# Norms by quarters: an encoder layer whose next stage begins on half of the early transposed pieces

## The reference

```python
x = layer_norm(ALPHA * x + 0.5 * swiglu(x, ffn1_w_up, ffn1_w_down), ln1_g, ln1_b)
h = mixer(x, ...)     # x @ w_in, short convolution, retention with 4 heads, gates, @ w_out
x = layer_norm(ALPHA * x + h, ln2_g, ln2_b)
x = layer_norm(ALPHA * x + 0.5 * swiglu(x, ffn2_w_up, ffn2_w_down), ln3_g, ln3_b)
```

## Time and profile before

| | |
|---|---|
| median of 3 runs | 1802.85 us (1801.83 to 1803.66) |
| the profiled execution itself | 1801.98 us, span 1799.8 us |
| PE busy | 1777.6 us, 99% |
| DVE, ACT, POOL busy | 1281.2, 645.0, 541.1 us |
| chain that ended last | PE 91%, DMA 3%, POOL 1%, DVE 1%, ACT 1% |
| granted PE clock | 0.997 of full speed |

### The profile page before, as it was taken

One profiled execution on the slowest core, in us unless ns is written; L12 is line 12 of the kernel. 1 busy time (PEld: TensorE's weight loads), 2 busy tenths in 40 slices (PEclk: granted clock), 3 DMA queues, 4 the chain that ended last, 5 costly groups with the idle time before them and its releaser, 6 DMA issues.

```text
span 1799.8 us, 26971 instructions
## 1 busy us (share of the span) xinstructions
PE 1777.6 (99%) x10868; PEld 1656.8 (92%) x10868; DVE 1281.2 (71%) x1698; ACT 645.0 (36%) x1102; POOL 541.1 (30%) x360
## 2 busy tenths in 40 slices
PE   9999999999999999999999999999999999999997
PEld 8989899898999999999998979798989989899896
DVE  7958485667798787776257666767867868485675
ACT  5425233242545454544106050514205325242242
POOL 2324242224232222121341323232244324233231
PEclk9999999999999999999999999999999999999998
DMA  7342423325443333422764958586964332323313
GB/s 272 129 141 71 141 73 132 123 71 199 146 143 127 115 130 101 143 87 91 273 240 140 339 200 312 204 284 231 345 258 158 129 135 77 129 82 129 114 63 106
DMA packets 89419, 287.33 MB, mean 160 GB/s; under 512 B 8784, under 2 KB 11216, under 8 KB 89040
## 3 DMA queue, kind: packets, MB, share of 16 engines
q1 hardware_dynamic: 48176, 171.72, 28.3%
q0 software_dynamic: 15552, 56.63, 9.2%
q10 hardware_dynamic: 25568, 57.26, 8.7%
HBM read 244.35 MB, written 42.28 MB: 159 GB/s over the span
## 4 chain that ended last, share of the span: by engine, by line
PE 91%; DMA 3%; POOL 1%; issue 1%; DVE 1%; ACT 1%; DVEq 0%; POOLq 0%
PE ps L771 90%; DMA wh<-in_weights 2%; PE ps L1141 1%; POOL wl L684 1%; DMA wh_x<-in_weights 1%; ACT xh L1282 0%; POOL wl_x L684 0%; DVE y L2075 0%; DVE z L2064 0%; PE ps L1084 0%; DVE y L2084 0%; ACT xin L1282 0%; DVE rt L1682 0%; DVE xl L1682 0%; DVE mv L2070 0%
## 5 line engine op out<-in xcount | busy, mean ns | idle before, releaser
L771 PE MATMUL ps<-th,wql 128*128 128x320 f32 x1136 | 350.9, 309 | 0.0
L771 PE MATMUL ps<-th,wqh 128*128 128x320 f32 x1136 | 350.7, 309 | 0.0
L771 PE MATMUL ps<-tl,wqh 128*128 128x320 f32 x1136 | 350.0, 308 | 0.0
L684 POOL TENSOR_TENSOR wl<-raw,wh 128x1024 fp32r<-128x1024 f32 x101 | 257.3, 2549 | 97.7 <-DMA wh<-in_weights 70.6
L1282 ACT ACTIVATE pu<-ps 128x320 f32<-128x320 f32 x213 | 93.3, 438 | 522.7 <-PE ps L771 522.6
L1682 DVE TENSOR_TENSOR wql<-qraw,wqh 128x512 fp32r<-128x512 f32 x213 | 259.9, 1220 | 17.3 <-ACT wqh L1282 17.1
L771 PE MATMUL ps<-xl,wqh 128*128 128x320 f32 x852 | 262.7, 308 | 0.0
L771 PE MATMUL ps<-xh,wqh 128*128 128x320 f32 x852 | 262.6, 308 | 0.0
L771 PE MATMUL ps<-xh,wql 128*128 128x320 f32 x852 | 262.5, 308 | 0.0
L697 POOL TENSOR_TENSOR quad_s<-qraw 128x512 f32<-128x512 f32 x71 | 93.7, 1319 | 485.2 <-DVE wql L1682 449.0
L1682 DVE TENSOR_TENSOR wql<-quad_s,wqh 128x512 fp32r<-128x512 f32 (+1 forms) x213 | 194.3, 912 | 45.3 <-ACT wqh L1282 44.5
(11 more groups left out here) (221 smaller groups left out, 3440.8 us busy)
## 6 DMA issues: line engine op xcount, KB each, us to landing
qraw<-in_quads SPq DMA_DIRECT2D x142, 512.0 KB, 3.6
raw<-in_weights SPq DMA_DIRECT2D x105, 512.0 KB, 3.8
wh<-in_weights POOLq DMA_DIRECT2D x101, 512.0 KB, 5.5
state<-in_state_ret ACTq DMA_DIRECT2D x32, 512.0 KB, 6.7
out_ret_sample<-state ACTq DMA_DIRECT2D x32, 512.0 KB, 5.2
state<-in_state_ret SPq DMA_DIRECT2D x16, 512.0 KB, 5.3
qk_scratch<-ctp SPq DMA_DIRECT2D x8, 640.0 KB, 5.4
swish_scratch<-ctp SPq DMA_DIRECT2D x6, 640.0 KB, 3.0
```

The lines of the kernel that those rows point to most:

```text
L684: pool.tensor_tensor(w_lo(r), w_raw(r), w_hi(r).bitcast(f32), ALU.subtract).then_inc(chunk_split, 1)
L771: ins = nc.tensor.matmul(out, lhs, rhs, start=start, stop=stop, skip_group_check=adds)
```

## The change

`FIRST_UNITS` goes from 3 to 4: four first halves stand ahead of the second halves, and the late tiles are transposed at k = 5 of the fourth unit. The idle products at the norms go. The early pieces are transposed in another order, and the first unit begins when the q = 0 pieces have high parts (`x_high`), with its products sorted by part. The first quad's operands are made inside the norm: POOL makes all four weight sums (`all_sums`) before the norm, ACT the six high parts, DVE the low parts at other places. The release order at the first norm, the place of one extra chunk slot, and the time of two quad loads and of two reloads of `z_kept` change with it.

```diff
-FIRST_UNITS = 3
+FIRST_UNITS = 4
-LATE_AT = (FIRST_UNITS - 1, 7)
+LATE_AT = (FIRST_UNITS - 1, 5)
-DOWN_LATE, OUT_LATE = (2, 0, 1, 3), (1, 0, 3, 4, 2)
-EXTRA_SLOT = {SECOND - DOWN_PARTS + 2: NSPL, SECOND: NSPL,
+DOWN_LATE, OUT_LATE = (3, 0, 2, 1), (1, 0, 3, 4, 2)
+EXTRA_SLOT = {SECOND - 1: NSPL, SECOND: NSPL,
+EARLY_PIECES = [(0, 0), (1, 0), (0, 1), (1, 1), (2, 0), (2, 1)]
+HIGH_ORDER = [(0, 0), (1, 0), (0, 1), (2, 0), (1, 1), (2, 1)]
+LOW_ORDER = [(t, q) for q in range(2) for t in range(EARLY)]
...
# SP, ahead of ffn(1)'s chunks (before: after its first three)
+            sync.wait_ge(merged_ready, KT)
+            for slot in range(4):
+                sync.wait_ge(state_out[slot], 32 * H)
+            load_quad(2)
+            load_quad(2)
             ffn(1)
...
# POOL
+            def all_sums(stage):
+                n = qk.at
+                sums(stage)
+                pool.wait_ge(pool_sums, 2 * n + 1)
+                pool.tensor_tensor(qs[:, 1, :], qs[:, 0, :], quad_source(n, A11), ALU.add).then_inc(later_sums, 1)
+                pool.wait_ge(later_sums, 2 * n + 1)
+                pool.wait_ge(quad_ready, operand(n - 1, S4))
+                pool.tensor_tensor(qs[:, 3, :], qs[:, 1, :], quad_source(n, A12), ALU.add).then_inc(later_sums, 1)
...
-                pool.wait_ge(z_ready, TT)
                 low()
+                pool.wait_ge(t_ready, 4 * 1 + 4)
                 sums(1)
...
             low()
+            all_sums(2)
             ffn(1)
...
# PE, to_T
-                if pieces is EARLY_PIECES:
-                    pe.wait_ge(x_low, kept + 1)
-                    pe.wait_ge(x_kept, kept + 1)
-                    idle_products(IDLE_UNITS, bk(-2 * EARLY) % 8)
+                if pieces is EARLY_PIECES:
+                    pe.wait_ge(psum_free, bk(EARLY - TT))
...
# PE, first_units
+                pe.wait_ge(x_kept, kept + 1)
+                for q in range(2):
+                    ks = range(4 * q, 4 * q + 4)
+                    pe.wait_ge(x_high, kept + HIGHS_BEFORE[q])
+                    for k in ks:
+                        products(0, 0, k, (0, 0), k == 0, False)
+                    pe.wait_ge(x_low, kept + EARLY * (q + 1))
+                    for k in ks:
+                        products(0, 0, k, (0, 1), False, False)
+                assert chunk() == s0
+                for k in range(KT):
+                    products(0, 0, k, (1, 0), False, k == KT - 1)
...
# ACT, end of the output product
+            act.wait_ge(psum_full, bk(EARLY))
+            for t in range(EARLY, TT):
+                kept_load(t)
+            for what in (A11, S12, A12, S3, A22, S4):
+                quad_hi_part(QUAD_START[2], what)
...
# DVE, x_sums: the wait for the first unit's chunk now stands before the second sum
+                    dve.wait_ge(chunk_used, released((SECOND, LAST)[stage - 1]))
                 tt(t3, b22, b12, ALU.subtract).then_inc(t_summed, 1)
...
# DVE, end_stage(k, ...)
+                if k == 1:
+                    quad_lo_part(PROJ, A11)
+                    quad_lo_part(PROJ, S12)
                 for t in early:
                     down(scale, 0, [t], residual)
                     moments(0, [t])
+                if k == 2:
+                    for what in (A11, S12, A12, S3, A22, S4):
+                        quad_lo_part(QUAD_START[2], what)
                 for t in early:
                     down(scale, 1, [t], residual)
                     moments(1, [t])
```

More of the change, by code:

```diff
@@ L1054, in ffn @@
                     idle_products(IDLE_START, 0)
-                for u in range(0 if first else FIRST_UNITS, 4):
-                    unit_of_chunk(x_wait=x_piece if first and u == 0 else None)
+                for u in range(FIRST_UNITS if first else 0):
+                    unit_of_chunk(x_wait=x_piece if u == 0 else None)
                 n = 0 if first else QUAD_START[2]
@@ L1103, in first_units, with products @@
                 own, kept = bk.at, (zr.at - EARLY) * 2
[L1104 to L1109, removed]
+                used = []
+                def products(u, half, k, which, start, stop):
+                    s, c = used[u], slice(half * HALF, (half + 1) * HALF)
+                    w_part, x_part = which
+                    w_of, x_of = (w_hi(s), w_lo(s))[w_part], (xh, xl)[x_part]
+                    return mm(ps[:, (own + 2 * u + half) % 8, 0:HALF], cols(k, 128, w_of), x_of[:, k, c], start, stop)
                 def late_tiles():
@@ new lines, in first_units @@
+                for u in range(FIRST_UNITS):
+                    pe.wait_ge(x_kept, kept + 2 * EARLY + u + 1)
+                    for k in range(KT):
+                        if u == 0 and k % 4 == 0:
+                            pe.wait_ge(x_low, kept + 2 * EARLY + (TT - EARLY) * (k // 4 + 1))
+                        products(u, 1, k, (1, 0), k == 0, False)
+                        products(u, 1, k, (0, 1), False, False)
+                        last = products(u, 1, k, (0, 0), False, k == KT - 1)
+                    last.then_inc(psum_full, 2)
+                    owed[0] = True
@@ L1331, in window @@
                 bk.add(2)
-                quad_hi_part(n, A11)
-                quad_hi_part(n, S12)
+                if ffn == 0:
+                    quad_hi_part(n, A11)
+                    quad_hi_part(n, S12)
                 plain_hi(2 * ffn)
-                for what in (A12, S3, A22, S4):
-                    quad_hi_part(n, what)
+                if ffn == 0:
+                    for what in (A12, S3, A22, S4):
+                        quad_hi_part(n, what)
                 act.wait_ge(psum_free, bk())
@@ L1483, in projections @@
                 x_hi_parts(1)
[L1484 to L1485 removed]
                 act.wait_ge(z_saved, 32)
[L1487 to L1492 removed]
+                for m in range(4):
+                    unit_gate(yr[:, m, :])
                 for q in range(len(PROJECTIONS)):
@@ L1659, in _ @@
         def _(dve):
-            bk, ad, st, hr, zr, root, lo = (Count() for _ in range(7))
+            bk, ad, st, hr, zr, root, lo, xc = (Count() for _ in range(8))
             V = nc.vector
@@ L1902, in projections @@
                 banks_freed(4)
-                for what in (A11, S12, A12, S3, A22, S4):
-                    quad_lo_part(n, what)
+                quad_lo_part(n, A22)
+                quad_lo_part(n, S4)
                 second_sum(n + 1)
@@ L2045, in end_stage @@
                 down(scale, 1, late, residual)
-                bk.add(2 * EARLY)
-                transposed_freed(k, early)
                 if residual is z:
```

202 lines of the change are left out of this document (111 added, 91 removed).

## The result

The changed kernel took 1806.98 us (median of 18 runs, 1805.86 to 1808.58), beside 1803.34 us (18 runs, 1801.53 to 1805.25) of the kernel before: ratio 1.0021, 95% interval 1.0015 to 1.0027. It is 3.6 us slower. The forecast was 1804.7, with a range of 1800.8 to 1808.5: the time lies inside, the sign was right, and the time was 2.3 us short of what was measured. As a difference it was +1.8 against +3.6; the other 0.5 is the kernel before, which took 1803.34 beside the changed one and 1802.85 in the first runs. That the time lies inside says little, since the range also held the time of the kernel before, that is, no change at all.

A forecast was written before the change was run, and what follows sets the result against it. PE's waits and idle products at the two norms, 8.2 us in all, were taken as all that could be won. First norm -3.4 and second norm +5.2 gave +1.8: 1804.7 us on the median, range 1800.8 to 1808.5.

The forecast's parts named there:

- Steps 1 and 2: First norm: the 0.87 us wait at 416.75 goes; PE may begin at 438.45, stream as if begun at 438.7, against 441.49.
- Step 3: First norm, late transposes: POOL's fourth low part delays DVE's last late tile about 1.1 us; cost 0.4 (0 to 1.3).
- Step 4: First norm: second halves begin at 455.15 and the first quad at 469.2, against 472.6 before.
- The sentence on the tile scaling: First norm: DVE's tile scaling, with two SBUF inputs, would stand still until POOL's low part ends, as already summed.
- The chain: Second norm: POOL's sums, ACT's copy and DVE's low parts take 8.6 us after POOL's last low part; DVE 5.1 late.
- The term c: Second norm: early quad loads make the last output chunk's low part end later, by 0 to 2.9 us, taken as 2.0.
- Even on time tiles it would give back only about 0.4: Second norm: with tiles on time, the change would win only about 0.4 us there.
- The loads did disturb: Answers the rival that quad loads before the second norm do not disturb, c near 0: 1802.6, chance 0.22.
- DVE was not in time: Answers the rival that the second norm's six low parts find operands in time, DVE free by about 1339: 1799.1, chance 0.08.
- The load rival in its strong form: Output product: two last chunks late by over 3 us each, PE waits there too: +5 to +8, 1809, chance 0.05.
- PE goes cold: Rival, second norm: waits without idle products bring a cold start, 2.15 us more or above: about 1807, chance 0.20.
- The sum: Both norms: -3.4 and +5.2 give +1.8, 1803.8 in the profiled execution's terms, 1804.7 on the median.

The follow-up runs named there:

- kernel 2: The changed kernel with only DVE's six low parts of the second norm moved back behind first_down's adds: 1800.84 us, ratio 0.9987.
- Kernel 6: The changed kernel with the first norm's store of the early z tiles issued only once all five tiles are done: 1806.03 us, ratio 1.0018.
- kernel 3: The changed kernel with two ring slots exchanged from the first norm's third unit's chunk on: 1805.57 us, ratio 1.0017.
- kernel 8: Kernel 1 with the ring's slots exchanged and the store of the early tiles later: 1800.18 us, ratio 0.9984.
- Kernel 9: Kernel 1 with POOL's fourth low part behind the late tiles and PE taking that unit's low-part products last: 1799.53 us, ratio 0.9982.
- kernel 1: The changed kernel with the second norm's first quad operands made and loaded at their old places: 1800.21 us, ratio 0.9984.
- kernel 4: The kernel before with the second norm's four quad loads issued early, as the change does: 1804.52 us, ratio 1.0008.
- kernel 5: The kernel before without its idle products at the norms and the two waits ahead of them: 1803.76 us, ratio 1.0002.

## Why the prediction was right, and where it was off

**First norm, predicted -3.4, measured -1.96.**
- Steps 1 and 2 held: no wait at 416.75, the first product at 438.45 as forecast.
- Step 3 is the term that was mis-sized. It let POOL run its four low parts in a row, priced the collision at 1.1 us of DVE's time and 0.4 of PE's, and called "a whole low part less PE's slack" the upper bound. The fourth `wh` was issued at about 436, next to the other loads of the last release and a 1.5 MB store, and landed after 11.4 us. So PE waited 1.26 for a weight part, a wait that the steps did not have at all; DVE was held as well, for 2.12 us. The cost of the step was 453.13 - 451.45 = 1.68 us instead of 0.4, above its upper bound of 1.3, and that is nearly all that the first norm fell short by. How late the load is varies: in kernel 2, whose first norm is the same program, the low part began at 445.75 instead of 447.53, and then held DVE's scaling of the first late tile instead. Kernel 6, whose load was there in time, shows that the store had made it late, and kernels 3, 6 and 8 that an earlier load alone only moves the collision to another instruction. Kernel 9 takes both away, and its trace is 1.3 us shorter in this norm.
- Step 4 held: from the late transposes to the first quad's copy it took 19.59 us, and 23.08 before, one half unit (3.52) less.
- The sentence on the tile scaling held. The row has 3.40 us beside a low part and 1.28 without. The Trainium skill (SBUF — State Buffer, "SBUF: two separate sides") gives the reason as an exclusive lock, for DVE operations with two SBUF inputs or in a mode that uses both ports; the small `rt<-mv` (2.16 us against 0.17) has one input, so only the second half of that rule could cover it. The trace agrees for the scaling, which stood until the low part ended. It also has an instruction with one input from SBUF that was not held, the moments of the late tiles: four in 2.47 us, of which 1.95 lie beside the low part that ends at 443.63.

```profile
441.68 2.47 DVE L2065 BATCH_NORM_STATS2 stats<-z 128x6 f32<-128x512 f32 x4
```

**Second norm, predicted +5.2, measured +6.5 (from quad to quad).**
- The chain was right to the tenth: from the low part's end (1335.96) to DVE's first add (1344.48) 8.5 us, forecast 8.6. PE waited at the early transposes for `z` and again before `first_down` for `hl`, as announced.
- The term c was mis-sized. Taken as 2.0 out of 0 to 2.9, it was 3.6: the low part began at 1333.57 in a kernel 1.96 ahead, against 1331.92. Its load took 7.3 us instead of 3.9, and the one ahead of it was late too, which the bound left out. With 3.6 in its place the prediction's own sum gives 3.2 + 3.6 = 6.8. For the same reason DVE's add did not come at the 1340 to 1342 that were announced, but at 1344.48; with c at 3.6 and the real lead of 1.96 the steps give 1342.9 + 3.6 - 1.96 = 1344.5.
- "Even on time tiles it would give back only about 0.4" fits kernels 1, 8 and 9, whose second norms are 0.2 to 0.3 us shorter than before from the first transpose to the first quad.

**The rivals.** The loads did disturb (kernel 4). DVE was not in time. The load rival in its strong form (both last chunks over 3 us late) did not come, though PE's waits for POOL in the output product rose from 0.4 to 1.5. *PE goes cold* was half right, and I had not seen how it would come: the clock did fall in the changed kernel, at the end of the wait for `z`, as the windows of the second norm show:

```profile
1356.00:1356.50 0.50, 0.00 (x0) 1.00 0.20 66
1356.50:1359.50 3.00, 2.73 (x13) 0.50 0.00 0
1359.50:1360.00 0.50, 0.50 (x5) 0.59 0.00 0
1360.00:1362.00 2.00, 1.21 (x12) 1.00 0.00 0
```

That is why the transposes took 4.34 us instead of 2.78. It cost nearly nothing, because the third tile was only done at 1359.35 and its eight transposes had to wait for that; in kernel 6 the clock stayed at 1.00 at the same place, behind a wait of 2.75 us (the row is below), and from the transposes to the first quad it took 54.00 us, against 53.94 in the changed kernel. The products behind came at full speed.

**The sum** was +1.8 in the traces' terms. Measured are +4.54 at the first quad of FFN 2 and 3.6 between the medians. Both terms erred the same way, by 1.4 and 1.3, so the errors added up. The difference of the medians lies closer to the forecast than the traces do, which is luck and not a merit of the sum; of the 0.9 between them I can say only that it is within what single executions scatter. That the change is slower was given 0.25 and that it is the same 0.67; the ratio came out at the line between them.

## What to carry over

When work is moved ahead of a critical step on an engine's queue, add up the whole chain that releases it, and put it behind the critical step if any link of it ends late: here the same six low parts cost 4.7 us in one place and nothing that the traces show in another. A load made early takes its time from the load that is awaited, so it should stand behind the last awaited one, as in kernel 1, and the bound on a load's delay has to include the loads ahead of it. And before an instruction of POOL is made earlier, look at what DVE does in the stretch where it will then run: the way out, in the trace of kernel 9, was to make it later, and to have PE take the products that don't need it first.

## What was not expected of the hardware

- The idle products have a use where the gap is long: without them, in kernel 5, PE stood 2.47 us and then ran 12 products at half the clock (0.267 us each instead of 0.147) at both norms. With a gap of 0.78 us, as in the changed kernel's first norm and in kernels 1, 8 and 9, the clock stayed at 1.00. After 2.79 us in the changed kernel it fell, and in kernel 3 too; after 2.75 us in kernel 6 it did not, so the length of the gap alone does not decide. The Trainium skill (TensorE: Matmul & The Clock Gate, Part 1) says that the clock falls after idling; the traces of kernel 5 and of the changed kernel agree, now with rows from mid-kernel. The row of kernel 6:

```profile
1355.63 1.97 PE L1115 MATMUL ps<-ident,z 128*128 128x128 f32 x16 [2.75 <-DVE z L2031]
```

- A DVE instruction on 128 x 2 numbers was held for 2.16 us beside a low part of POOL, against 0.17 alone, and for 1.56 us in kernels 6 and 8. Each time it ended with the low part: how small the held instruction is doesn't matter.
- A 512 KB load took 3.9 us to land on nearly empty queues, 7.3 beside four quad loads, and 11.4 beside three loads and a store of 1.5 MB.
